# First column quarter of the last output stage made inside the last delta head of a four-mixer encoder kernel

## The reference, cut to what matters

```
def _odd_mixer(h, w_in, ..., w_out, Sg0, Sd0, buf0):
    ...
    hd, Sd = _gdn_chunked(qd, kd, _heads(vd, D_HEADS), g, beta, Sd0)
    o = jnp.concatenate([_head_rmsnorm(hc), _head_rmsnorm(hd)], axis=-1) * g_head
    z = jax.nn.silu(jnp.concatenate([zc, zd], axis=-1).astype(F32))
    return (o * z) @ w_out, ...
```

## Time and profile before

| | us |
|---|---|
| median of 3 runs (lowest, highest) | 1605.67 (1605.19, 1609.41) |
| the profiled execution: its time | 1610.02 |
| the profiled execution: its span, first to last instruction | 1608.2 |
| TensorE (matmul) busy | 1514.3, 94% |
| VectorE busy | 979.7, 61% |
| ScalarE busy | 628.3, 39% |
| GpSimd busy | 180.8, 11% |
| mean granted TensorE clock, share of full | 0.973 |

### The profile page before, as it was taken

One profiled execution on the slowest core, in us unless ns is written; L12 is line 12 of the kernel. 1 busy time (PEld: TensorE's weight loads), 2 busy tenths in 40 slices (PEclk: granted clock), 3 DMA queues, 4 the chain that ended last, 5 costly groups with the idle time before them and its releaser, 6 DMA issues. The chain is left out here.

```text
span 1608.2 us, 30737 instructions
## 1 busy us (share of the span) xinstructions
PE 1514.3 (94%) x11056; PEld 1415.6 (88%) x11056; DVE 979.7 (61%) x2122; ACT 628.3 (39%) x1491; POOL 180.8 (11%) x384
## 2 busy tenths in 40 slices
PE   6999999999999999799799999899999999977998
PEld 2689999998999999799699999899999998966998
DVE  2666565665867767733576664577677667754622
ACT  2523232322232332423564442355555455543521
POOL 1000000000000000001000001023222312312000
PEclk9999999999999999899799999999999999988899
DMA  9343433441552433233441502311211121020223
GB/s 335 107 115 95 110 95 108 102 126 39 118 154 80 116 103 99 63 97 101 119 83 50 130 21 63 96 43 46 71 44 55 44 59 41 6 74 4 89 89 118
DMA packets 195260, 141.01 MB, mean 88 GB/s; under 512 B 18332, under 2 KB 178584, under 8 KB 194916
## 3 DMA queue, kind: packets, MB, share of 16 engines
q1 hardware_dynamic: 177772, 130.22, 28.6%
q10 hardware_dynamic: 17400, 9.60, 2.2%
HBM read 128.65 MB, written 11.15 MB: 87 GB/s over the span
## 5 line engine op out<-in xcount | busy, mean ns | idle before, releaser
L182 PE MATMUL bank<-hT,w_high 128*128 128x288 f32 x1152 | 361.4, 314 | 6.0 <-ACT retention_qkT_raw L1272 2.1
L183 PE MATMUL bank<-hT,w_low 128*128 128x288 f32 x1152 | 342.7, 298 | 0.0
L184 PE MATMUL bank<-hT,w_high 128*128 128x288 f32 x1152 | 342.7, 297 | 0.0
L182 PEld LDWEIGHTS bank<-hT,w_high 128*128 128x128 f32 x1152 | 220.5, 191 | 7.6 <-DVE w_low L974 2.9
L183 PEld LDWEIGHTS bank<-hT,w_low 128*128 128x128 f32 x1152 | 220.3, 191 | 0.0
L184 PEld LDWEIGHTS bank<-hT,w_high 128*128 128x128 f32 x1152 | 219.6, 191 | 0.0
L182 PE MATMUL bank<-output_w_split,gT_high 128*128 128x256 f32 x512 | 143.4, 280 | 0.0
L184 PE MATMUL bank<-output_w_split,gT_high 128*128 128x256 f32 x512 | 143.2, 280 | 0.0
L183 PE MATMUL bank<-output_w_split,gT_low 128*128 128x256 f32 x512 | 142.7, 279 | 0.0
L183 PEld LDWEIGHTS bank<-output_w_split,gT_low 128*128 128x128 f32 x512 | 96.6, 189 | 0.0
L182 PEld LDWEIGHTS bank<-output_w_split,gT_high 128*128 128x128 f32 x512 | 96.3, 188 | 0.1
(11 more groups left out here) (491 smaller groups left out, 3589.2 us busy)
## 6 DMA issues: line engine op xcount, KB each, us to landing
x<-in_w_in_even SPq DMA_DIRECT2D x72, 512.0 KB, 5.3
x<-in_w_in_odd SPq DMA_DIRECT2D x56, 512.0 KB, 4.5
x<-in_w_ada SPq DMA_DIRECT2D x32, 256.0 KB, 4.7
front_w_ada<-in_w_ada SPq DMA_DIRECT2D x6, 1024.0 KB, 15.6
output_w_raw<-in_w_out_even SPq DMA_DIRECT2D x12, 512.0 KB, 3.4
output_w_raw<-in_w_out_odd SPq DMA_DIRECT2D x12, 512.0 KB, 3.5
gdn_E<-G_rows SPq DMA_DIRECT2D x8, 576.0 KB, 5.1
gT<-in_w_ada SPq DMA_DIRECT2D x16, 256.0 KB, 3.4
```

What stands on the lines that cost most here:

```text
L182: pe.matmul(out, w[0], x[1], start=first, stop=False)
L183: pe.matmul(out, w[1], x[0], start=False, stop=False)
L184: return pe.matmul(out, w[0], x[0], start=False, stop=last)
```

## The change

Of the output product of layer 1, the first column quarter (q = 0) moves into the delta heads. Fifteen of its sixteen K slices (all but slice 15, which is head 7's own result) are multiplied in the last turn, at the cuts where other turns have `project`. The 60 prompt steps (15 slices x 4 tiles, three matmuls of 256 columns each) are cut by a table of their own, `LAST_FILL`. The sample has a step of two matmuls for each slice; eight of them stand between the last three `turn_g`. The new stage `output_last` replaces `output` for layer 1: it finishes q = 0 (slice 15 for all tiles, slices 8 to 15 for the sample) and does q = 1 to 3 as before, with the tiles of q = 0 held in PSUM banks 0, 1 and 3 and the others in banks 4 to 7.

The splits that these steps need move with them. In turn 6, weight groups 0 and 1 (four slices, 1024 columns wide each) and slices 0 to 4 of gT are split during the recurrence; in turn 7 weight groups 2 and 3, slices 5 to 14 and the sample pair. Layer 1's `g_high` lies where head 7's projection still reads its input, so the high parts of slices 0 to 4 go to buffers that are free by then ("homes": the level masks, AT, k_beta_decay, kT) and are copied to their place in turn 7 (`act_keep`), before head 7 writes those buffers. The two transposes of the convolution cache move from banks 0 and 1 to bank 7, behind the second fill. The weights of q = 1 are loaded into the place of those of q = 0 as soon as these are split. GpSimd's loop runs over seven heads, and its eighth turn is written out with one wait more.

```diff
+class OutputAhead:
...
+    def act_keep(self, act, tiles):
+
+        for k in tiles:
+            act.wait_ge(*self.g_high.done(0, k))
+            act.activation(self.M.g_high[1][:, k, 0:SEQ], self.homes[k], ACT.Copy).then_inc(self.kept.sem, 1)
...
+    def tile_step(self, pe, k, t, last=False):
...
+        pe.matmul(out, g[0], w[1], start=(k == 0 and t < 2), stop=False, skip_group_check=True)
+        pe.matmul(out, g[1], w[0], start=False, stop=False, skip_group_check=True)
+        return pe.matmul(out, g[0], w[0], start=False, stop=last, skip_group_check=True)
...
+    FILL = ((0, 5, 24, 28, 36, 38), LEVEL_FILL, END_FILL)
+    LAST_FILL = ((0, 5, 26, 30, 36, 38), ((38, 39, 40, 41, 42, 44), (44, 45, 46, 47, 48, 50), (50, 50, 51, 51, 52)),
+                 ((52, 53, 54), (54, 55, 56), (56, 57, 58), (58, 59, 60), (60, 60, 60)))
...
+        def fill(pe, h, a, b):
+
+            if h is not None:
+                project(pe, h, a, b)
+            else:
+                if a == 0:
+                    pe.wait_ge(*s["proj_copied"].before(H, 0))
+                out.pe_tiles(pe, a, b)
...
-            project(pe, ahead, 0, 5)
+            fill(pe, ahead, start_fill[0], start_fill[1])
...
@@ act_turn, recurrence over t @@
+                if ahead is None and t == 0:
+                    out.act_pair(act)
+                elif ahead is not None and second is None:
+                    if t == 0:
+                        act.wait_ge(*s["level_ready"].done(h, NL - 1))
+                        out.act_w(act, 1)
+                    out.act_g(act, t, t + 1)
...
@@ dve_turn, recurrence over t @@
+                if ahead is not None and second is None:
+                    if t in (1, 3):
+                        out.dve_w(dve, t // 2)
+                    if t:
+                        out.dve_g(dve, t - 1, t)
+                elif ahead is None and t == 1:
+                    out.dve_pair(dve)
...
@@ output_last, TensorE @@
+                def finish_first():
+                    for k in range(SAMPLE_DONE, done):
+                        ahead.sample_step(pe, k)
+                    pe.wait_ge(*g_lo.done(0, 0))
+                    for t in range(PT):
+                        ahead.tile_step(pe, done, t, True).then_inc(y_psum.sem, 1)
+                    pe.wait_ge(*g_lo.done(0, 1))
+                    ahead.sample_step(pe, done, True).then_inc(y_psum.sem, 1)
...
+                finish_first()
+                for q in range(1, NQ):
+                    for pos in range(T):
+                        multiply(q, pos)
```

More of the change, by code:

```diff
@@ L1930, in pe_turn @@
                     last.then_inc(s["N_psum"].sem, 1)
-                project(pe, ahead, fill[0], fill[1])
+                fill(pe, ahead, steps[0], steps[1])
                 for i in range(2):
@@ L1938, in pe_turn @@
                     last.then_inc(s["Z_psum"].sem, 1)
-                project(pe, ahead, fill[1], fill[2])
+                fill(pe, ahead, steps[1], steps[2])
                 for i in range(2):
@@ L1944, in pe_turn @@
                     last.then_inc(s["ZZ_psum"].sem, 1)
-                project(pe, ahead, fill[2], fill[3])
+                fill(pe, ahead, steps[2], steps[3])
                 for i in range(2):
@@ L1950, in pe_turn @@
                     last.then_inc(s["YY_psum"].sem, 1)
-                project(pe, ahead, fill[3], fill[4])
+                fill(pe, ahead, steps[3], steps[4])
                 if inner:
@@ L1958, in pe_turn @@
                         last.then_inc(s["X_psum"].sem, 1)
-                    project(pe, ahead, fill[4], fill[5])
+                    fill(pe, ahead, steps[4], steps[5])
             pe.wait_ge(*s["kv_scaled"].done(h, 0))
@@ L1998, in pe_turn @@
                     turn_g(pe, h, t - 2)
-                project(pe, ahead, *END_FILL[t][1:3])
+                fill(pe, ahead, *end_fill[t][1:3])
+                if ahead is None and t == T - 1:
+                    out.pe_sample(pe, SAMPLE_FILL[0], SAMPLE_FILL[1])
         def act_turn(act, h, ahead, second):
@@ L2005, in act_turn @@
                     high(act, ahead, 1)
+                    if ahead is None:
+                        act.wait_ge(*s["proj_psum"].before(H, 0))
+                        act.wait_ge(*s["gT_copied"].before(H - 2, 0))
+                        out.act_g(act, 5, 7)
                 act.wait_ge(*s["tok_psum"].done(h, t))
@@ L2018, in act_turn @@
             act.wait_ge(*s["kq_psum"].done(h, 0))
+            if ahead is None:
+                act.wait_ge(*out.kept.done(0, 0))
             for i, x in enumerate((kT, qT)):
@@ L2054, in act_turn @@
                     take_projection(act, ahead, 5)
+                    if ahead is None:
+                        out.act_g(act, 12, 14)
                     for t in range(T):
@@ L2061, in act_turn @@
                     high(act, second, 0)
+                    if ahead is None:
+                        act.wait_ge(*s["gT_copied"].before(H - 1, 0))
+                        out.act_g(act, 14, 15)
+                    elif second is None:
+                        act.wait_ge(*s["proj_psum"].done(ahead, 5))
+                        out.act_w(act, 0)
                 for i in range(2) if n < NL - 1 else ():
@@ L2110, in dve_turn @@
             low(dve, ahead, 1)
+            if ahead is None:
+                out.dve_g(dve, 5, 7)
             dve.wait_ge(*s["tok_squared"].done(h, 0))
@@ L2166, in dve_turn @@
             dve.wait_ge(*s["scale_b"].done(h, 0))
+            if ahead is None:
+                dve.wait_ge(*out.kept.done(0, 4))
             dve.tensor_tensor(kbe[:], tk[:, :, 1, :], spread(sc[:, 2, :]), ALU.mult).then_inc(s["kv_scaled"].sem, 1)
@@ L2223, in dve_turn, with pool_turn @@
             take_g(T - 1)
-        def pool_turn(pool, h):
+            if ahead is not None and second is None:
+                out.dve_g(dve, T - 1, T)
+        def pool_turn(pool, h, last=False):
             pool.wait_ge(*s["ss_ready"].done(h, 0))
@@ L2231, in pool_turn @@
             pool.wait_ge(*s["A_ready"].done(h, 0))
+            if last:
+                pool.wait_ge(*out.kept.done(0, 3))
             for n in range(NL):
@@ L2264, in _ @@
                     load_G(h - 1)
+                for ct in range(3):
+                    sp.wait_ge(*s["w_split_low"].done(H - 1, ct))
+                    out.load(sp, ct)
+                load_G(H - 1)
                 sp.wait_ge(*s["w_split_low"].done(H - 1, 3))
-                load_G(H - 1)
-                first.start(sp)
+                out.load(sp, 3)
+                for j in range(3):
+                    out.load_next(sp, j)
                 for i, name in enumerate(("pconv", "sconv")):
```

351 lines of the change are left out of this document (329 added, 22 removed).

## The result

| | before | changed |
|---|---|---|
| median of 4 runs, us | 1607.49 | 1585.85 |
| lowest and highest, us | 1605.19, 1609.41 | 1581.27, 1587.45 |
| ratio to before, 95% interval | | 0.9861, 0.9835 to 0.9888 |
| profiled execution, us | 1610.0 | 1581.27 |
| its span, us | 1608.2 | 1579.4 |

The change is faster, by 1.4%: 22 us where I had forecast 27. The measured 1585.85 us lies 1.35 us above the top of my range. Of the level, 1.8 us is the kernel before, whose median was 1605.67 us when the forecast was made and is 1607.49 over four runs; the rest is the change itself. So the forecast had the sign and most of the size right, and the size is still wrong by more than I allowed for.

What follows compares the result with a forecast made beforehand. TensorE was taken as the bound nearly everywhere, except in the last turn and the output stage's first quarter. Terms -28.7, -1.9 and +3.5 sum to -27.1 us, giving 1578.6 us; forecast 1575.5 to 1581.5, chance 0.60, wider range 1573.0 to 1584.5.

Steps and rivals of the forecast that it cites:

- The output stage, -28.7 us: Output stage loses its first quarter: quarter 1's first matmul in effect 3.8 us after the start instead of 32.5.
- Turn 6, +3.5 us: Turn 6's recurrence: splits ahead of u on ScalarE, and VectorE's excesses, lengthen it by 3.5 us, bounds 1.5 and 5.5.
- The clock: Sign in the changed profile: TensorE's clock at 1.0 from turn 7's start to its end; 0.5 after the seam means rival 2.
- rival 2: TensorE's clock falls again around the last transposes, quarter 1 starts at 1.2 GHz: +2.9 us, 1581.5; chance 0.08.
- Turn 7, -1.9 us: Turn 7 with fills, reckoned from turn 6: 54.45 us against 56.3, bounds 50.5 and 56.3.
- the other added work of turn 7: Turn 7's added splits, copies and DMAs: costed at nothing, each with its cover; a failed one delays under 1 us.
- VectorE's weight group and slice 7 (1.22 + 0.61) stand in the 2.15 us in which it waits for GpSimd's power: Turn 7, before the norms: these VectorE splits fit in its wait for GpSimd and cost nothing.
- Up to the norms nothing changes (0.57 us of wait there grows by 0.1): Start of turn 7, against turn 6: TensorE's wait for the norms grows by only 0.1 us.
- The late splits in the levels replace the longer convolutions: Turn 7's levels: late splits take the place of the next head's convolutions and cost nothing.
- The other four covers: Turn 7: ScalarE's splits, VectorE's three slices, copies ahead of X and sample steps cost nothing, the last at most 0.2 us.
- number 1: Splits cost more: VectorE's excesses in series, GpSimd held, one turn 7 cover failing by 1 us; 1581.5 to 1584.5; chance 0.15.
- Rival 4: Turn 7's fills don't hide: 1623.7 in series at 1.2 GHz, 1602.1 at full clock; chance 0.03, 0.01 for slower.

Runs made afterwards that it cites:

- series version: Changed kernel with turn 7's 60 tile steps made in one piece behind its last tile, all splits where they were: turn 7 64.4 us, kernel 1610.26 us.
- gap version: Changed kernel with turn 6's splits spread and ScalarE's slices 1 to 4 between its copies of u and output: turn 6 55.57 us, kernel 1579.85 us.
- spread version: Changed kernel with turn 6's splits moved to where ScalarE or VectorE idles: turn 6 57.11 us, kernel 1585.20 us.
- version with early slices: Changed kernel with ScalarE rounding slices 11 to 14 right behind 7 to 10 in turn 7, not in the levels: turn 7 56.87 us, kernel 1582.96 us.
- norms freed: Changed kernel with VectorE's two splits moved out of its wait for GpSimd's power in turn 7: turn 7 58.17 us, kernel 1584.82 us.
- copies with one input: Changed kernel with VectorE's two splits in the wait for GpSimd's power made plain one-input copies: turn 7 57.77 us, kernel 1585.78 us.

## Why the prediction was right and where it was wrong

**The output stage, -28.7 us: right.** Quarter 1 began 3.4 us after the stage's start and has some 0.3 us of waits for its first groups, 3.7 in all against 3.8 forecast. The seam itself is unchanged. From the first sample step to quarter 1 it is 7.20 to 7.23 us in both profiles of the changed kernel and in every version but the one in series.

**Turn 6, +3.5 us: right.** It is 3.1 and 3.3 us in the two profiles. The slots were put at 1.5, 0.5, 0.5, 0.8 and 0.2 and measured at 1.5, 0.4, 0.5, 0.4 and 0.2. The reason given for them, ScalarE without idle time ahead of u, is shown by the gap version, which takes the slices from there and leaves 0.3 us. The reason given for the fourth, VectorE's excess, was the wrong one: the slot kept its 2.64 us in the spread version, where VectorE has no weight group there, and only once ScalarE's slice was gone did VectorE's share show, at 0.3 us. That is the one slot whose size was off, by 0.4.

**The clock: right.** Up in turn 7, the seam and the stage, so rival 2 didn't happen. The series version shows that it is the fills that hold it. But it fell once, in the version with early slices, at the norms' wait. So the rival was nearer than my 0.08 suggested, in a place that I had not named.

**Turn 7, -1.9 us: wrong, +2.9 in the first profile and +2.0 in the second.** Against the 54.45 us forecast the first profile has 59.2. The step that failed is the one on "the other added work of turn 7", which I had costed "at nothing, each with its cover", and within it two covers out of six:

- "VectorE's weight group and slice 7 (1.22 + 0.61) stand in the 2.15 us in which it waits for GpSimd's power". They don't stand in it, they shut GpSimd out, and the wait begins behind them. With this cover fell the step "Up to the norms nothing changes (0.57 us of wait there grows by 0.1)": the wait came to 2.29 us. Cost 1.73 us in the first profile and 0.84 in the second, by the norms freed; the shorter copies with one input at the same place cost 0.3.
- "The late splits in the levels replace the longer convolutions". They do so in length and not in what they wait for. A convolution needed only its own input; a slice's low part needs ScalarE to have rounded it, and ScalarE came to that behind its Z evictions. Cost 3.65 us, which the early slices gave back with no other change. With them the levels were 7.31, 7.21 and 5.29 us, within 0.1 of the 7.3, 7.2 and 5.4 of the sum.

These two are 5.4 us in the first profile. The norms without splits came 0.25 us earlier than forecast (12.05 for 12.3) and the recurrence took 0.2 less, which leaves about the 4.75 that was missing. The other four covers (ScalarE ahead of k and q, the three slices behind the decay matrix, the copies ahead of X, the sample steps) held: the stretch from the k transposes to the first level is 9.8 us, in turn 6 9.9.

I had also written that a failed cover delays "by its excess, under 1 us each". This was the second fault, and it made the range too narrow. It assumed that a cover that fails fails by what it is short in length. Neither did: the first failed by exclusion, at up to its whole length, the second by order, at the length of another engine's queue.

What hurts is that the row was at hand. I had weighed the exclusion of GpSimd and VectorE, with the Trainium skill, for turn 6, where it costs little because the norm is wanted a tile later. I did not carry it to the one place where VectorE waits for GpSimd by name, two paragraphs above. Even the 0.54 us of the operation on the means in the kernel before looks like a held one: in its turn 6 it starts 0.46 us before the end of VectorE's silu and ends 0.08 us behind it.

The rivals: number 1 had the mechanism ("GpSimd held, one cover in turn 7 failing"), with the cover priced at 1 us, and the measured time lies 1.35 us above its end. Rival 4's 1602.1, the fills in series at full clock, was tried: 1610.26, as the turn then runs at the lower clock.

## What to carry to other kernels

An engine's wait is room for other work only if that work leaves alone what the engine waits for. Before a wait is counted as a cover, ask which engine ends it, and where GpSimd ends a wait of VectorE, whether the inserted instruction shuts GpSimd out; here splits with two SBUF inputs did, and a copy with one did too. And for each inserted instruction ask what it itself waits for and what is queued behind it: a split that is short enough still costs the whole wait for its other half. Within a loop of tiles the same 0.6 us of work cost 0.4 to 0.5 us a tile ahead of the recurrent value, and 0.3 us in all four tiles together in the wait just behind it.

## What the runs showed of the hardware

- GpSimd's operation on 128 x 10 numbers took 0.54 us beside one VectorE operation with two SBUF inputs, 2.28 us beside three back to back, whose last ended 0.08 us before it. Of the six profiles with splits in that place it waited out the whole row in two; in the four where it slipped in, the next one was stretched from 1.97 to 2.80 us, up to 1.82 us behind the end of the 1.22 us split. A copy of 0.70 us with one SBUF input in place of that split stretched it to 2.28, up to 1.81 us behind the copy's end. VectorE's own times (1.22, 0.68 to 0.70) didn't change with which of GpSimd's operations they met.
- Perhaps the other way round too: of two VectorE products of 128 x 5 numbers beside GpSimd's masks of 128 x 128, the first took 1.38 to 1.73 us in turn 7 of the ten profiles, the second 0.15 to 0.33 in nine and 1.80 in the version with the norms freed. That it is a wait for GpSimd is read from the times and not shown by a run.
- A wait of TensorE of 2.3 us left the granted clock at 2.4 GHz in the changed kernel and let it fall to 1.2 in the version with early slices, which has the same instructions on TensorE ahead of it. What decided there is open.
